# Splitting the final normalisation of the last rows between GpSimd, VectorE and ScalarE in a hybrid decoder step

## The reference

```
def rmsnorm(x, g):
    y = xf * lax.rsqrt(jnp.mean(xf * xf, axis=-1, keepdims=True) + EPS)
    return (y * g.astype(jnp.float32)).astype(x.dtype)
...
        xp = xp + ffn(rmsnorm(xp, norm_ffn_g[l]), w_up[l], w_down[l])
        xs = xs + ffn(rmsnorm(xs, norm_ffn_g[l]), w_up[l], w_down[l])
...
    y_prompt = rmsnorm(xp, norm_f_g)
```

## Time and profile before

| | us |
|---|---|
| median of 3 runs | 2528.41 |
| the 3 runs | 2526.08, 2528.41, 2528.50 |
| profiled execution, its own time | 2530.2 |
| its span | 2528.4 |

### The profile page before, as it was taken

One profiled execution on the slowest core, in us unless ns is written; L12 is line 12 of the kernel. 1 busy time (PEld: TensorE's weight loads), 2 busy tenths in 40 slices (PEclk: granted clock), 3 DMA queues, 4 the chain that ended last, 5 costly groups with the idle time before them and its releaser, 6 DMA issues.

```text
span 2528.4 us, 36243 instructions
## 1 busy us (share of the span) xinstructions
PE 2462.6 (97%) x13683; PEld 2249.5 (89%) x13683; DVE 1398.4 (55%) x2478; ACT 696.4 (28%) x1424; POOL 217.1 (9%) x383
## 2 busy tenths in 40 slices
PE   6999999999899999899999999999999999999997
PEld 4899999999788888789899998988888988989986
DVE  5535654586766666654445545446645455454545
ACT  4333331211444443412122121213321211212213
POOL 3100011000233333100000000000100000000002
PEclk9999999999799999999999999999999999999999
DMA  4123244322744444611111111112411111111101
GB/s 145 51 76 104 85 130 123 126 75 97 238 141 142 139 140 131 213 34 59 41 50 50 40 59 33 55 45 67 150 51 34 60 40 44 56 33 50 50 25 75
DMA packets 219131, 212.22 MB, mean 84 GB/s; under 512 B 32252, under 2 KB 190304, under 8 KB 215692
## 3 DMA queue, kind: packets, MB, share of 16 engines
q1 hardware_dynamic: 219028, 210.84, 26.8%
HBM read 161.11 MB, written 49.79 MB: 83 GB/s over the span
## 4 chain that ended last, share of the span: by engine, by line
PE 55%; DVE 2%; POOL 1%; issue 1%; ACT 0%; DMA 0%; DVEq 0%; POOLq 0%; ACTq 0%
PE bank L122 18%; PE bank L124 18%; PE bank L123 18%; PE bank L2153 1%; PE bank L2151 1%; DVE f_h_lo L2058 0%; PE bank L2197 0%; DVE f_acc L2001 0%; DVE f_acc L152 0%; POOL ff_rs L101 0%; DVE xn L2047 0%; POOL ff_rt L108 0%; POOL ff_rt L109 0%; DMA xn<-x_dram 0%; POOL ff_rs L111 0%
## 5 line engine op out<-in xcount | busy, mean ns | idle before, releaser
L2001 DVE TENSOR_TENSOR f_acc<-bank,f_acc 128x512 f32<-128x512 f32 x512 | 351.6, 691 | 297.1 <-PE bank L124 297.0
L122 PE MATMUL bank<-f_h_hi,f_up_lo 128*128 128x344 f32 (+1 forms) x1536 | 490.9, 320 | 2.3 <-DVE f_h_lo L2058 2.2
L124 PE MATMUL bank<-f_h_hi,f_up_hi 128*128 128x344 f32 (+1 forms) x1536 | 489.8, 319 | 0.0
L123 PE MATMUL bank<-f_h_lo,f_up_hi 128*128 128x344 f32 (+1 forms) x1536 | 489.5, 319 | 0.0
L122 PE MATMUL bank<-f_dn_hi,f_z 128*128 128x512 f32 x1024 | 399.3, 390 | 0.5 <-DVE x_s L2001 0.5
L124 PE MATMUL bank<-f_dn_hi,f_z 128*128 128x512 f32 x1024 | 398.8, 389 | 0.0
L123 PE MATMUL bank<-f_dn_lo,f_z 128*128 128x512 f32 x1024 | 398.8, 389 | 0.0
L122 PE MATMUL bank<-h_hi,w_lo 128*128 128x412 f32 (+3 forms) x1000 | 351.7, 352 | 0.8 <-DVE w_lo L724 0.8
L123 PE MATMUL bank<-h_lo,w_hi 128*128 128x412 f32 (+3 forms) x1000 | 350.6, 351 | 0.0
L124 PE MATMUL bank<-h_hi,w_hi 128*128 128x412 f32 (+3 forms) x1000 | 350.4, 350 | 0.0
L2016 DVE TENSOR_TENSOR f_sqr<-f_relu 128x344 f32<-128x344 f32 (+1 forms) x192 | 99.1, 516 | 360.7 <-ACT f_relu L1938 359.3
(11 more groups left out here) (380 smaller groups left out, 2889.3 us busy)
## 6 DMA issues: line engine op xcount, KB each, us to landing
up_raw<-in_w_up_dram SPq DMA_DIRECT2D x64, 512.0 KB, 4.7
f_dn_raw<-in_w_down_dram SPq DMA_DIRECT2D x64, 512.0 KB, 3.4
p_dram<-ffn_gains SPq DMA_DIRECT2D x24, 1024.0 KB, 4.6
up_raw<-in_w_in_dram SPq DMA_DIRECT2D x24, 512.0 KB, 5.1
up_raw<-p_dram SPq DMA_DIRECT2D x48, 256.0 KB, 5.1
xn<-p_dram SPq DMA_DIRECT2D x32, 256.0 KB, 5.0
xres<-in_x_prompt_dram SPq DMA_DIRECT2D x16, 512.0 KB, 4.8
x_dram<-x SPq DMA_DIRECT2D x16, 512.0 KB, 3.1
```

Of the source, the lines that this page charges most:

```text
L122: pe.matmul(out, wl, xh, start=start and k == 0, stop=False, skip_group_check=skip)
L123: pe.matmul(out, wh, xl, start=False, stop=False, skip_group_check=skip)
L124: last = pe.matmul(out, wh, xh, start=False, stop=stop and k == n - 1, skip_group_check=skip)
L2001: dve.tensor_tensor(dst, bank, dst, ALU.add).then_inc(s["y_added"], 1)
```

## The change

GpSimd makes only the root of tiles 0 and 1 and then multiplies tiles 2 to 6 by the weights, each as soon as it has been squared. VectorE scales tile 0 behind add 11 and tile 1 behind add 13, makes the root of tiles 2 to 5 behind add 14, and after add 17 multiplies the already weighted tiles 2 and 3 by their roots, makes the root of tiles 6 and 7 and scales tile 7. ScalarE, after its last square, multiplies tiles 4, 5 and 6 by their roots. The stores keep their order 0 to 7.

```diff
@@ SyncE
-            for m in range(NBT):
+            for m, made, count in ((0, out_made[1], 1), (1, out_made[1], 2), (2, out_made[1], 3), (3, out_made[1], 4),
+                                   (4, s["rows_scaled"], 1), (5, s["rows_scaled"], 2), (6, s["rows_scaled"], 3), (7, out_made[1], 5)):
+                row = BLK + m * P
                 eng.wait_ge(stored[m % IN_PLACE], 16 * (2 + m // IN_PLACE))
-                store_rows(1, m)
+                eng.wait_ge(made, count)
+                eng.dma_start(io["y_prompt"][0, row:row + P, :], slot(1, m)).then_inc(stored[m % IN_PLACE], 16)
@@ GpSimd
-            for pair in range(NBT // 2 - 1):
-                finals[1].scales(pool, pair, 2 * pair)
+            finals[1].scales(pool, 0, 0)
+            for m in range(2, 7):
+                row = slot(1, m)
+                pool.wait_ge(finals[1].squared, m + 1)
+                pool.tensor_tensor(row, row, fgain[:], ALU.mult).then_inc(s["rows_gained"], 1)
@@ ScalarE
             for m in range(NBT):
                 finished_square(1, m)
+            for m in range(4, 7):
+                act.wait_ge(s["rows_gained"], m - 1)
+                act.wait_ge(s["last_refined"], (1 if m < 6 else 2) * DVE_RSQRT_STEPS)
+                act.activation(slot(1, m), slot(1, m), ACT.Copy, scale=finals[1].rs[:, m:m + 1]).then_inc(s["rows_scaled"], 1)
@@ VectorE
+            def last_roots(n, first, after):
+                last, cols = finals[1], slice(first, after)
+                dve.wait_ge(last.squared, after)
+                dve.tensor_scalar(last.ms[:, cols], last.ss[:, cols], 1.0 / D, EPS, ALU.mult, ALU.add).then_inc(s["last_ms_made"], 1)
+                dve.wait_ge(s["last_ms_made"], n + 1)
+                dve_rsqrt(dve, s["last_refined"], n * DVE_RSQRT_STEPS, last.rs[:, cols], last.ms[:, cols], last.rt[:, cols])
...
-                elif u in (13, 15):
-                    finish(1, u - 13)
-                    finish(1, u - 12)
-            finish(1, NBT - 4)
-            finish(1, NBT - 3)
-
-            last = finals[1]
-            cols = slice(NBT - 2, NBT)
-            dve.wait_ge(last.squared, NBT)
-            dve.tensor_scalar(last.ms[:, cols], last.ss[:, cols], 1.0 / D, EPS, ALU.mult, ALU.add).then_inc(s["last_ms_made"], 1)
-            dve.wait_ge(s["last_ms_made"], 1)
-            dve_rsqrt(dve, s["last_refined"], 0, last.rs[:, cols], last.ms[:, cols], last.rt[:, cols])
-            for m in range(NBT - 2, NBT):
+                elif u == 11:
+                    finish(1, 0)
+                elif u == 13:
+                    finish(1, 1)
+                elif u == 14:
+                    last_roots(0, 2, 6)
+
+            for m in (2, 3):
                 row = slot(1, m)
-                dve.scalar_tensor_tensor(out=row, in0=row, scalar=last.rs[:, m:m + 1], in1=fgain[:],
-                                         op0=ALU.mult, op1=ALU.mult).then_inc(out_made[1], 1)
+                dve.wait_ge(s["rows_gained"], m - 1)
+                dve.tensor_scalar(row, row, finals[1].rs[:, m:m + 1], None, ALU.mult).then_inc(out_made[1], 1)
+            last_roots(1, 6, NBT)
+            row = slot(1, NBT - 1)
+            dve.scalar_tensor_tensor(out=row, in0=row, scalar=finals[1].rs[:, NBT - 1:NBT], in1=fgain[:],
+                                     op0=ALU.mult, op1=ALU.mult).then_inc(out_made[1], 1)
```

More of the change, by code:

```diff
@@ L1763, in ffn @@
     names = """up_loaded0 up_loaded1 dn_loaded up_hi_made up_lo_made dn_hi_made dn_lo_made z_ready relu_made zhi_made
-        sqr_made zlo_made y_ready y_added fgain_loaded z_padded low_moved s_summed s_final s_stored last_ms_made last_refined""".split()
+        sqr_made zlo_made y_ready y_added fgain_loaded z_padded low_moved s_summed s_final s_stored last_ms_made last_refined rows_gained rows_scaled""".split()
     s = {nm: sem("f_" + nm) for nm in names}
@@ L1832, in load_in_place, with store_rows @@
                 eng.dma_start(xn[:, i % XN, :], io["x1_dram"][row:row + P, :]).then_inc(xn_loaded[i % XN], 16)
[L1834 to L1837, removed]
+            def store_rows(m):
+                eng.wait_ge(out_made[0], m + 1)
+                eng.dma_start(io["y_prompt"][0, m * P:(m + 1) * P, :], slot(0, m)).then_inc(stored[m % IN_PLACE], 16)
             def up_weights(tn, p, up):
@@ L1877, in _ @@
                     for m in range(IN_PLACE):
-                        store_rows(0, m)
+                        store_rows(m)
                     down_weights(NTL, 1)
@@ L2051, in finish @@
                 row = slot(blk, m)
-                finals[blk].scaled(dve, m // (IN_PLACE if blk == 0 else 2), m, row, row, fgain).then_inc(out_made[blk], 1)
+                finals[blk].scaled(dve, m // IN_PLACE, m, row, row, fgain).then_inc(out_made[blk], 1)
+            def last_roots(n, first, after):
[4 more added lines that the diff above has]
+                dve_rsqrt(dve, s["last_refined"], n * DVE_RSQRT_STEPS, last.rs[:, cols], last.ms[:, cols], last.rt[:, cols])
             def cut_lo(i):
```

## The result

| | before | changed |
|---|---|---|
| median of 10 runs each | 2529.15 us | 2534.51 us |
| lowest, highest | 2525.43, 2531.91 | 2532.59, 2536.28 |
| profiled execution, its own time | 2530.2 | 2534.4 |
| its span | 2528.4 | 2532.7 |
| TensorE's last product ends | 2513.09 | 2512.54 |

The account below looks back on a forecast made before the run. The prediction took the kernel as TensorE-bound, with only the tail behind its last product open to change. Held port time moved the last store's landing from 2527.2 to 2531.0: 2528.4 + 3.8 = 2532.2, rounded to 2532; range 2525 to 2535.

Parts of the forecast that it names:

- step 3: VectorE's early root (columns 2 to 5): 2.2 us alone, plus two GpSimd products of 2.2 coming between; taken to end at 2518.7.
- step 4: Adds 15 to 17 queue behind the early root on VectorE; last one ends at 2520.5, now 2515.55.
- step 6: VectorE scales rows 2 and 3, about 0.65 us each, beside GpSimd's row 6 product of 2.2; done at 2524.0.
- step 7: VectorE's last root (columns 6 and 7) queues behind the scalings of rows 2 and 3; 2.1 us, ending at 2526.1.
- step 8: VectorE scales row 7 until 2527.4; ScalarE scales row 6 from 2526.1 to 2527.15.
- step 9: SyncE issues row 6's store at 2527.2, row 7's 0.33 later; they land at 2529.8 and 2531.0.
- The rival that made it dearer by plain doubling: GpSimd's product takes 2.60 or more, nothing fixed in it; over +5 us; chance 0.22, shared with several more holds.
- both far bounds: Limits for GpSimd's 128x1024 product: 1.88 us recorded below, 2.98 above.
- steps 1 and 2: Row 0's scaling, row 2's product, row 1's scaling, row 3's product alternate on the port from 2505.9 to 2512.7.
- the band over +5: Outcome more than 5 us slower, through a dearer product or several holds more; chance 0.22.
- The rival in which VectorE keeps the port through its root: No handover inside the early root, which ends at 2514.9; +3.6 us, 2532; counted within the forecast's 0.62.
- the fast one: Small operations and row scalings run beside GpSimd, stores bind: -3.3 us, 2525; chance 0.12 for -3.3 to +2, 0.04 beyond.

Follow-up runs that it names:

- late_root: The changed kernel with the early root (rows 2 to 5) behind add 17 instead of add 14; tail 19.1 us, ratio 1.0018.
- no_products: The changed kernel without GpSimd's five products, the weights of rows 2 to 6 left out of the result; tail 11.8 us, ratio 0.9989.
- store_order: The changed kernel with rows 4 and 5 stored ahead of row 3; tail 19.4 us, ratio 1.0013.
- one_late_root: The kernel before with one VectorE root for rows 4 to 7, earlier scalings of rows 0 to 3, no GpSimd products; tail 13.3 us, ratio 0.9987.

## Why the prediction was right, and by how much it missed

By its own steps, each from the end of TensorE's last product (predicted with 2513.1, measured with 2512.54):

| step | predicted | measured |
|---|---|---|
| GpSimd's product, unhindered / waiting | 2.40 / 3.4 | 2.40 / 3.39 |
| early root ends (step 3) | 5.6 | 5.9 |
| last add ends (step 4) | 7.4 | 7.9 |
| rows 2 and 3 scaled (step 6) | 10.9 | 11.3 |
| last root ends (step 7) | 13.0 | 13.3 |
| row 7 scaled (step 8) | 14.3 | 14.7 |
| last store issued (step 9) | 14.4 | 15.1 |
| last store lands | 17.9 | 19.0 |
| tail | 19.1 | 20.2 |

*The price* was right, from a 128x512 form with its fixed part taken off. That it fits to the hundredth is luck: the row that it was taken from (L1479, 1.30) isn't of two plain tensors, as the prediction says, but repeats its weights for each head. The plain one, L1457 at 1.27, gives 2.34 by the same sum. The rival that made it dearer by plain doubling (2.60) is out, and so are both far bounds. Behind another product, with nothing in between, a product is recorded with 2.33.

The estimate of 2.3 that the prediction works out from the Trainium skill, GPSIMD Engine Reference, section "3.1 Elementwise — side-by-side cycle accounting", whose figure is for an add, is 0.1 too low for a product that starts alone.

*The mechanism* was right: alternation for whole instructions, in the root too, though the two waiting operations took 1.71 and 2.26 and not both over 2. The first is shorter because it came late to its product: row 1's scaling ended at 2512.17, add 14 ran beside the third product, and the root's first operation was issued at 2512.69, 0.5 us after that product could start. In late_root, where it stands behind add 17, it took 2.23.

*The order in steps 1 and 2* was wrong, the sum was not. I let row 0's scaling go first, then row 2's product. The product won (3.52 against 2.40), so rows 2 and 3 had their products before row 1 was scaled. Four products and two scalings hold the port before the root is through in either order, so it still ended within 0.3 of the forecast.

*The mis-sized term is the store pile in step 9.* I took only rows 6 and 7 as touching and let the last land 3.5 after its own issue. Row 3's scaling ends 0.55 behind the fifth product, rows 4 and 5 were ready but stand behind row 3 in SyncE's order, and five stores run into one another. Measured: 3.9 from the last issue, and 0.43 in place of 0.33 between the last two issues. The other half of the miss is in the engine steps: row 6's store was issued 14.6 us after the last product where 14.1 was forecast, 0.1 of it from ScalarE's 1.15 in place of 1.05. Together these make the 1.1 by which the tail missed.

*The time* was forecast as 2532.2, rounded to 2532, and came out at 2534.51, only 0.5 below the range's upper end. The median before, over ten runs, is 0.7 above the 2528.41 that I started from, and the tail adds 1.1; where the remaining 0.5 is, if it is more than scatter, no profile shows. By the ratio's 5.8 the result even lies in the band over +5 that I had given to a dearer product, though the product was not dearer.

*The rival in which VectorE keeps the port through its root* is out by the two long operations; *the fast one* described not the change but no_products: 3.3 us shorter than before was forecast for it, a tail shorter by 3.5 came, with the stores as the limit, as it said.

## What to carry to other kernels

Work that goes from VectorE to GpSimd leaves VectorE only if VectorE has nothing with two SBUF inputs (or a row scaling, or a small chain) to do meanwhile: add up the port time of both engines, here 2.2 us held for a GpSimd product against 1.2 for the scaling that it was to shorten or replace. A GpSimd product belongs beside operations with an input in PSUM, which kept their 0.69 here. Where a chain of small dependent operations has a fixed price (2.2 us for 2 columns as for 4), make it once for all rows that are ready, and look at which store waits in the queue behind another.

## What the runs showed of the hardware that was not expected

Who gets the port can't be read from the recorded starts alone. Row 0's scaling is recorded from 2505.29 and the product from 2505.34, and the product had the port; late_root (2506.95 and 2506.99) went the same way, with 3.52 again. It isn't the size of GpSimd's operation that decides. Two pairs with operations on two columns, the first from store_order, the second from one_late_root:

```profile
2503.06 1.30 DVE L152 SCALAR_TENSOR_TENSOR x_s<-x_s,ffs_rs,ffn_gains 8x1024 f32<-8x1024 f32 x1
2503.10 0.20 POOL L109 TENSOR_TENSOR ff_rt<-ff_rt,ff_ms 128x2 f32<-128x2 f32 x1
2503.38 1.04 POOL L110 TENSOR_SCALAR ff_rt<-ff_rt 128x2 f32<-128x2 f32 x1
...
2506.37 1.28 DVE L152 SCALAR_TENSOR_TENSOR f_acc<-f_acc,ff_rs,ffn_gains 128x1024 f32<-128x1024 f32 x1
2506.42 1.28 POOL L145 TENSOR_SCALAR ff_ms<-ff_ss 128x2 f32<-128x2 f32 x1
```

In the first VectorE's row leads by 0.04, and GpSimd's operation goes through unhindered (0.20). VectorE's takes 1.30 where it took 1.26 in the changed kernel, and only GpSimd's next one is held (1.04). In the second it leads by 0.05, and GpSimd is held (1.28). Over all these runs, GpSimd went first at every lead of 0.04 and VectorE at every one of 0.06 or more (before the change, 0.13: 2508.30 against GpSimd's 2508.43, held for 1.20). At 0.05 both occur.

This is also what shifts the first product by 0.2 us between runs. GpSimd's first root meets the scaling of the sample rows; where GpSimd goes first there, its root loses 0.85 us (1.04 in place of 0.19), and otherwise 1.05 to 1.07 (1.25 to 1.27 in place of 0.20).

The Trainium skill, SBUF — State Buffer, section "Who interferes with whom", gives the pair to whoever issues first. By the recorded starts this case disagrees at leads of 0.04 and 0.05 us; the measured 3.52 decides. Whether a recorded start is the moment of issue, no run here shows.

ScalarE's copy with a scale for each row took 1.15 in place where I took 1.05 from its plain copies.
